# Recurrent mixer of a float32 transformer stack: products moved to GpSimd, decay scales folded into ScalarE's exponentials, one gate chunk moved behind the block products

## Chip, cores and metric

The kernel runs on one core of a Trainium2 chip. The metric is the device time of one launch in microseconds (us); three runs were timed, and lower is better.

## What is computed

A residual stream x of 256 positions by 1024 channels, float32, goes through a first block of two layers (an attention mixer with a convolutional feed-forward part, then a recurrent mixer with another such part) and through two layers of a second block. The change touches the recurrent mixer alone:

```
def odd_mixer(x, w_in, conv_w, conv_b, w_a, b_a, w_x, b_x, lam, w_out):
    gate_branch, xr = jnp.split(x @ w_in, 2, axis=-1)
    xr = causal_dwconv(xr, conv_w, conv_b)
    xb = xr.reshape(bsz, seq, RG_BLOCKS, RG_BLOCK_W)
    r = jax.nn.sigmoid(jnp.einsum('bsnc,ncd->bsnd', xb, w_a).reshape(bsz, seq, D_RNN) + b_a)
    i = jax.nn.sigmoid(jnp.einsum('bsnc,ncd->bsnd', xb, w_x).reshape(bsz, seq, D_RNN) + b_x)
    log_a = (-LRU_C * r.astype(jnp.float32)) * jax.nn.softplus(-lam.astype(jnp.float32))
    a = jnp.exp(log_a)
    u = jnp.sqrt(-jnp.expm1(2.0 * log_a)) * (i * xr).astype(jnp.float32)
    _, h = lax.associative_scan(lru_combine, (a, u), axis=1)
    y = h.astype(x.dtype) * jax.nn.gelu(gate_branch)
    return y @ w_out
```

## The kernel before

**Layout.** Channels lie on the 128 partitions, so an activation is 8 tiles of 128 by 256. Every operand of a matmul is split in two parts that TensorE takes in its fast float32 form: a rounded high part (written by ScalarE) and the low rest (written by VectorE). One product then takes three matmuls: high times high (line 247), high weights times low activation (line 248), low weights times high activation (line 249).

**The weight stream.** Weights come from HBM as a stream of 1 MB chunks (16 blocks of 128 by 128) in the order in which TensorE uses them. SyncE loads chunk n into one of three raw buffers as soon as the low part of chunk n-3 is written. ScalarE rounds it to `w_hi` (line 220, "high refill"), once the chunk four places ahead of it has been multiplied; VectorE writes `w_lo`, the difference (line 229, "low refill"). Both have a ring of four slots. Where these two refills stand in the order of ScalarE and VectorE is written out by hand; each engine runs its list in order and waits on semaphores.

**The stage around the change.** TensorE multiplies four chunks for the recurrent branch xr, one gate chunk (`od_gate0`), two chunks of block products (`od_ax`, eight steps j that give the arguments of r and i, each with two tiles), three more gate chunks and then the output projection `od_out`. Its first two chunks are taken together (`alternating`, lines 287 and 294): first all products with the high part of y, tile by tile as `yhi0` to `yhi3` come, then all with the low part (`ylo0` to `ylo3`). It waits at its start for the low refills of both chunks. VectorE scales the xr and gate products out of PSUM (line 314), adds three taps of the convolution (1431), writes the low part of the result (1437), multiplies r by the decay coefficient (1466, "la") and i by xr (1468, "ux"), finishes the argument of the root (1478, "v"), forms u (1486), scans (1491, two tiles for each pair h), multiplies by the gate (1497, "y") and takes the low part (1502, "ylo"). ScalarE has the last tap (1070), the high part of xr (1076), the sigmoids (1086), then for each pair of tiles Exp, Tanh and Square (1131, 1132, 1135), the roots (1138), the GELUs (1091) and the high part of y (1096, "yhi"). Each time another family of functions is needed, an ACT_TABLE_LOAD comes first. GpSimd does nothing in this stage; in the feed-forward parts of the first block it multiplies (760) and subtracts (766), in the second block it works at lines 1527 and 1530.

## Time and profile before

| quantity | value |
|---|---|
| median of 3 runs | 1929.05 us (1927.96 to 1929.65) |
| span of the profiled execution, first to last instruction | 1926.9 us |
| TensorE busy, matmuls | 1861.4 us (97%) |
| VectorE busy | 1394.7 us (72%) |
| ScalarE busy | 970.6 us (50%) |
| GpSimd busy | 141.2 us (7%) |
| mean granted TensorE clock | 0.984 of full speed |

The profile holds one execution. The page gives its span but no time of its own around that span; the median of the timed runs is 2.15 us longer than the span. Times in the rows are microseconds from the span's start. The recurrent mixer lies between about 386 and 478 us. PE is TensorE's matmuls, PEld its weight loads, DVE is VectorE, ACT is ScalarE, POOL is GpSimd. A row's idle time in brackets is what the engine spent waiting just before it, and on whom.

### The profile page before, as it was taken

What the parts mean: (1) busy time and instruction counts of PE and PEld (TensorE: products, weight loads), DVE (VectorE), ACT (ScalarE), POOL (GpSimd) and SP (SyncE); (2) the same over time, 40 slices, a digit from 0 to 9 for tenths busy, and PEclk for the clock granted to TensorE, in tenths of its full rate; (3) what the DMA queues carried; (4) which work ended last, traced back from release to release, by engine and by line L of the source; (5) the groups of instructions that cost most, each with busy time, mean ns of one, the idle gap of its engine ahead of it and who ended that gap; (6) DMA issues with size and microseconds to landing.
All of it is one profiled execution on the core that took longest, in us unless ns stands there. A gap on an engine that the chain in (4) does not pass through costs nothing.

```text
span 1926.9 us, 31805 instructions
## 1 busy us (share of the span) xinstructions
PE 1861.4 (97%) x13316; PEld 1749.7 (91%) x13316; DVE 1394.7 (72%) x1704; ACT 970.6 (50%) x1177; POOL 141.2 (7%) x128
## 2 busy tenths in 40 slices
PE   7978999998999999999999999999999999999997
PEld 7958999998999898889999988898889999998887
DVE  5796998578799557756775677757775686577774
ACT  5453755367665445544453455535554445355552
POOL 0020332000233000000300000000000020000000
PEclk9989999999999999999999999999999999999999
DMA  7413455534454445564455545553556345445551
GB/s 282 151 44 120 176 187 185 197 133 173 168 196 184 179 149 191 180 219 153 167 200 181 175 147 181 201 214 132 190 187 219 147 175 193 158 153 197 181 214 64
DMA packets 46788, 334.66 MB, mean 174 GB/s; under 512 B 5184, under 2 KB 5568, under 8 KB 6464
## 3 DMA queue, kind: packets, MB, share of 16 engines
q1 hardware_dynamic: 46512, 332.20, 47.9%
q8 instruction: 105, 1.72, 0.4%
q0 software_dynamic: 144, 0.52, 0.1%
q14 instruction: 27, 0.22, 0.0%
HBM read 331.65 MB, written 1.05 MB: 173 GB/s over the span
## 4 chain that ended last, share of the span: by engine, by line
PE 88%; DVE 7%; ACT 2%; DMA 1%; issue 1%; SPq 0%; DVEq 0%; ACTq 0%
PE psum L263 25%; PE psum L266 12%; PE psum L247 12%; PE psum L248 12%; PE psum L249 12%; PE psum L287 6%; PE psum L294 3%; DVE w_lo L229 2%; PE psum L334 1%; PE psum L506 1%; DMA w_raw<-stream_in 1%; PE psum L509 1%; PE psum L508 1%; PE psum L356 1%; DVE scratch L1318 0%
## 5 line engine op out<-in xcount | busy, mean ns | idle before, releaser
L220 ACT ACTIVATE w_hi<-w_raw 128x2048 fp32r<-128x2048 f32 x313 | 597.9, 1912 | 460.1 <-PE psum L249 223.7
L229 DVE TENSOR_TENSOR w_lo<-w_raw,w_hi 128x2048 fp32r<-128x2048 f32 x313 | 717.8, 2297 | 55.7 <-ACT w_hi L220 55.7
L247 PE MATMUL psum<-x_split,w_hi 128*128 128x256 f32 x1768 | 504.3, 285 | 10.7 <-DVE x_split L372 10.4
L248 PE MATMUL psum<-x_split,w_hi 128*128 128x256 f32 x1768 | 501.4, 284 | 0.0
L249 PE MATMUL psum<-x_split,w_lo 128*128 128x256 f32 x1768 | 501.4, 284 | 0.0
L263 PE MATMUL psum<-x_split,w_hi 128*128 128x512 f32 x1216 | 429.8, 399 | 0.0
L247 PEld LDWEIGHTS psum<-x_split,w_hi 128*128 128x128 f32 x1768 | 340.5, 193 | 12.0 <-issue 10.9
L266 PE MATMUL psum<-x_split,w_lo 128*128 128x256 f32 x1216 | 341.5, 281 | 0.0
L248 PEld LDWEIGHTS psum<-x_split,w_hi 128*128 128x128 f32 x1768 | 340.6, 193 | 0.1
L249 PEld LDWEIGHTS psum<-x_split,w_lo 128*128 128x128 f32 x1768 | 340.5, 193 | 0.0
L263 PE MATMUL psum<-h_split,w_hi 128*128 128x512 f32 x816 | 288.6, 399 | 0.0
L263 PEld LDWEIGHTS psum<-x_split,w_hi 128*128 128x128 f32 x1216 | 228.5, 188 | 57.0
L266 PEld LDWEIGHTS psum<-x_split,w_lo 128*128 128x128 f32 x1216 | 229.7, 189 | 0.0
L266 PE MATMUL psum<-h_split,w_lo 128*128 128x256 f32 x816 | 229.2, 281 | 0.0
L263 PEld LDWEIGHTS psum<-h_split,w_hi 128*128 128x128 f32 x816 | 153.3, 188 | 38.2
L266 PEld LDWEIGHTS psum<-h_split,w_lo 128*128 128x128 f32 x816 | 154.2, 189 | 0.0
L314 DVE TENSOR_TENSOR scratch<-psum,inv_rms 128x512 f32<-128x512 f32 (+1 forms) x129 | 87.0, 684 | 79.4 <-PE psum L249 79.2
L663 ACT ACTIVATE scratch<-psum 128x512 f32<-128x512 f32 x76 | 45.4, 598 | 195.0 <-PE psum L266 195.0
L247 PE MATMUL psum<-h_split,w_hi 128*128 128x256 f32 x480 | 138.9, 289 | 4.5 <-DVE h_split L1395 2.5
L249 PE MATMUL psum<-h_split,w_lo 128*128 128x256 f32 x480 | 137.3, 286 | 0.0
L248 PE MATMUL psum<-h_split,w_hi 128*128 128x256 f32 x480 | 137.3, 286 | 0.0
L308 DVE TENSOR_TENSOR scratch<-psum,scratch 128x512 f32<-128x512 f32 x76 | 52.6, 692 | 103.7 <-ACT scratch L663 103.7
(215 smaller groups left out, 2376.5 us busy)
## 6 DMA issues: line engine op xcount, KB each, us to landing
w_raw<-stream_in SPq DMA_DIRECT2D x313, 1024.0 KB, 4.8
x_resid<-x_in SPq DMA_DIRECT2D x1, 1024.0 KB, 6.9
y_out<-x_resid SPq DMA_DIRECT2D x4, 256.0 KB, 2.5
scratch<-mask_in SPq DMA_DIRECT2D x1, 768.0 KB, 11.0
scratch<-ev_in SPq DMA_DIRECT2D x1, 512.0 KB, 9.5
scratch<-inv_in POOLq DMA_DIRECT2D x1, 512.0 KB, 4.5
params<-par_in SPq DMA_DIRECT2D x1, 247.0 KB, 7.1
matrices<-mat_in SPq DMA_DIRECT2D x1, 192.0 KB, 8.9
```

Of the source, the lines that this page charges most:

```text
L220: act.activation(w_hi[:, n % RING, :], raw[:, n % RAWS, :], ACT.Copy).then_inc(hi_ready, 1)
L229: dve.tensor_tensor(w_lo[:, n % RING, :], raw[:, n % RAWS, :], w_hi[:, n % RING, :].bitcast(F32), ALU.subtract).then_inc(lo_ready, 1)
L247: pe.matmul(dst, w_hi[:, c.slot, b:b + P], src[:, k0 + k, 0, :], start=opens, stop=False)
L248: pe.matmul(dst, w_hi[:, c.slot, b:b + P], src[:, k0 + k, 1, :], start=False, stop=False)
L249: done = pe.matmul(dst, w_lo[:, c.slot, b:b + P], src[:, k0 + k, 0, :], start=False, stop=last and k == nk - 1 and m == len(tiles_) - 1)
L263: pe.matmul(ps[:, bank_, :], w_hi[:, c.slot, b:b + P], src[:, k0 + k, :, :].rearrange("p a t -> p (a t)"), start=first and k == 0, stop=False)
L266: done = pe.matmul(tile(bank_, 0), w_lo[:, c.slot, b:b + P], src[:, k0 + k, 0, :], start=False, stop=last and k == nk - 1)
L287: pe.matmul(tile(c.bank, m), w[:, c.slot, b:b + P], src[:, k0 + k, 0, :], start=k == 0 and m == 0 and w is w_hi, stop=False)
L294: done = pe.matmul(tile(c.bank, m), w_hi[:, c.slot, b:b + P], src[:, k0 + k, 1, :], start=False, stop=k == nk - 1 and m == 1)
L308: dve.tensor_tensor(dst, ps[:, c.bank:c.bank + 2, 0:T], S(ACC + 2 * c.slot, 2), ALU.add).then_inc(pair_taken, 2)
L314: dve.tensor_tensor(dst, bank(c.bank, tiles), rinv[:, :].unsqueeze(1).to_broadcast([P, tiles, T]), ALU.mult).then_inc(pair_taken, 1)
L663: act.activation(S(ACC + 2 * c.slot, 2), ps[:, c.bank:c.bank + 2, T:2 * T], ACT.Copy)\
```

## The change

Four things change, all in the recurrent mixer.

The gate chunk that stood ahead of the block products goes behind them, in the stream and in every engine's order, so there are now four `od_gate` chunks in a row. On VectorE the "la" multiplications go away: Exp and Tanh take the coefficient as a per-partition scale, one tile at a time, with two small extra operations that prepare the scales in the attention layer ahead. The "ux" products, three of the four "u" products and three of the four "ylo" subtractions go to GpSimd. And the refills are placed anew in the lists of ScalarE and VectorE.

```diff
-         ("od_xr", 4, 4), ("od_gate0", 1, 1), ("od_ax", 2, 0), ("od_gate", 3, 3), ("od_out", 4, 4),
+         ("od_xr", 4, 4), ("od_ax", 2, 0), ("od_gate", 4, 4), ("od_out", 4, 4),
...
@@ odd_act (ScalarE) @@
-            act.wait_ge(chunk_done, gate0.number + 1)
-            refill_hi(act, gate0)
             sigmoids(0)
...
-            refill_hi(act, Chunk("od_ax", 1))
             act.wait_ge(*A.after("i7"))
+            act.wait_ge(*ev_dve.after("l_pos"))
             for h in G4:
-                act.wait_ge(*od_dve.after(f"ux{2 * h + 1}"))
-                act.activation(S(TMP + 2 * h, 2), S(RR + 2 * h, 2), ACT.Exp).then_inc(*A.did(f"a{h}"))
-                act.activation(S(RR + 2 * h, 2), S(RR + 2 * h, 2), ACT.Tanh, scale=-1.0)\
-                   .then_inc(*A.did(f"tanh{h}"))
-                act.wait_ge(*A.after(f"a{h}"))
+                for j in (2 * h, 2 * h + 1):
+                    act.activation(S1(TMP + j), S1(RR + j), ACT.Exp, scale=small[:, 16 + j:17 + j])\
+                       .then_inc(*A.did(f"a{j}"))
+                    act.activation(S1(RR + j), S1(RR + j), ACT.Tanh, scale=small[:, 72 + j:73 + j])\
+                       .then_inc(*A.did(f"tanh{j}"))
+                act.wait_ge(*od_pool.after(f"ux{2 * h + 1}"))
+                act.wait_ge(*A.after(f"a{2 * h + 1}"))
                 act.activation(S(XC + 2 * h, 2), S(TMP + 2 * h, 2), ACT.Square).then_inc(*A.did(f"a2{h}"))
+                if h == 1:
+                    refill_hi(act, Chunk("od_ax", 1))
+                if h == 2:
+                    act.wait_ge(chunk_done, gate[0].number + 1)
+                    refill_hi(act, gate[0])
...
 VectorE, odd_dve
+            dve.wait_ge(*od_act.after("sqrt0"))
+            dve.wait_ge(*od_pool.after("ux1"))
+            dve.tensor_tensor(S(II, 2), S(II, 2), S(RR, 2), ALU.mult).then_inc(*V.did("u0"))
             scan(0)
-            take_scaled(dve, gate[1], S(GB + 4, 2))
+            take_scaled(dve, gate[2], S(GB + 4, 2))
             scan(1)
-            refill_lo(dve, gate[1])
             gated(0)
+            refill_lo(dve, gate[2])
+            scan(2)
             gated(1)
-            lo(0)
-            scan(2)
-            lo(1)
-            gated(2)
+            take_scaled(dve, gate[3], S(GB + 6, 2))
             scan(3)
-            take_scaled(dve, gate[2], S(GB + 6, 2))
-            lo(2)
+            gated(2)
             gated(3)
...
+        def odd_pool(pool):
+            for j in range(8):
+                pool.wait_ge(*od_act.after(f"i{j}"))
+                pool.tensor_tensor(S1(II + j), S1(II + j), S1(XC + j), ALU.mult).then_inc(*od_pool.did(f"ux{j}"))
+            for h in range(1, 4):
+                pool.wait_ge(*od_act.after(f"sqrt{h}"))
+                pool.wait_ge(*od_pool.after(f"ux{2 * h + 1}"))
+                pool.tensor_tensor(S(II + 2 * h, 2), S(II + 2 * h, 2), S(RR + 2 * h, 2), ALU.mult)\
+                    .then_inc(*od_pool.did(f"u{h}"))
+            for h in range(3):
+                pool.wait_ge(*od_act.after(f"yhi{h}"))
+                pool.tensor_tensor(hs[:, 2 * h:2 * h + 2, 1, :], S(GB + 2 * h, 2),
+                                   hs[:, 2 * h:2 * h + 2, 0, :].bitcast(F32), ALU.subtract)\
+                    .then_inc(*od_pool.did(f"ylo{h}"))
```

VectorE from the last root arguments (line 1478) to the first products of pair 0, in the program of before; 1486 is u, 1491 the scan, 314 a gate chunk taken out of PSUM, 229 a low refill, 1497 the product with the gate.

```order
L1478 SCALAR_TENSOR_TENSOR scratch<-scratch 128x512 x3
L1486 TENSOR_TENSOR scratch<-scratch 128x512
L1491 SCALAR_TENSOR_TENSOR scratch<-scratch 128x256 x2
L314 TENSOR_TENSOR scratch<-psum,inv_rms 128x512
L1486 TENSOR_TENSOR scratch<-scratch 128x512
L1491 SCALAR_TENSOR_TENSOR scratch<-scratch 128x256 x2
L229 TENSOR_TENSOR w_lo<-w_raw,w_hi 128x2048
L1497 TENSOR_TENSOR scratch<-scratch 128x512 x2
```

The same place in the changed program, where 1469 is the root argument, 1493 u of pair 0, 1482 the scan and 1488 the product with the gate.

```order
L1469 SCALAR_TENSOR_TENSOR scratch<-scratch 128x512 x2
L314 TENSOR_TENSOR scratch<-psum,inv_rms 128x512
L229 TENSOR_TENSOR w_lo<-w_raw,w_hi 128x2048
L1493 TENSOR_TENSOR scratch<-scratch 128x512
L1482 SCALAR_TENSOR_TENSOR scratch<-scratch 128x256 x2
L314 TENSOR_TENSOR scratch<-psum,inv_rms 128x512
L1482 SCALAR_TENSOR_TENSOR scratch<-scratch 128x256 x2
L1488 TENSOR_TENSOR scratch<-scratch 128x512
L229 TENSOR_TENSOR w_lo<-w_raw,w_hi 128x2048
```

A low refill now stands between the root arguments and u of pair 0, one u has left VectorE's list, and the other low refill (for the second chunk of the output projection) has moved from ahead of the first gate product to behind it.

ScalarE from the last sigmoids to the roots, in the changed program: 1085 is a sigmoid, 1128 Exp, 1130 Tanh, 1134 Square, 1142 the root, 220 a high refill.

```order
L1085 ACTIVATE scratch<-psum,params 128x256 x8
L1128 ACT_TABLE_LOAD
L1128 ACTIVATE scratch<-scratch,small 128x256
L1130 ACTIVATE scratch<-scratch,small 128x256
...
L1134 ACTIVATE scratch<-scratch 128x512
L220 ACTIVATE w_hi<-w_raw 128x2048
...
L1142 ACT_TABLE_LOAD
L1142 ACTIVATE scratch<-scratch 128x512 x4
```

Before, one high refill stood ahead of the table load and none between Exp and the roots; now none is ahead and two lie inside (behind pair 1 and behind pair 2), and sixteen operations on 128 by 256 take the place of eight on 128 by 512.

GpSimd between its last subtraction of one feed-forward part and its first product of the next, in the changed program.

```order
L766 TENSOR_TENSOR h_split<-scratch,h_split 128x256
L1514 TENSOR_TENSOR scratch<-scratch 128x256 x8
L1518 TENSOR_TENSOR scratch<-scratch 128x512 x3
L1522 TENSOR_TENSOR h_split<-scratch,h_split 128x2x256 x3
L760 TENSOR_TENSOR scratch<-scratch 128x256 x2
```

The fourteen rows of lines 1514 (ux), 1518 (u1 to u3) and 1522 (ylo0 to ylo2) are new there; before, line 760 followed upon line 766.

## Rows read from the trace of the kernel before

**Rows 1.** The page, busy time of each engine: us, share, instructions.

```profile
PE 1861.4 (97%) x13316; PEld 1749.7 (91%) x13316; DVE 1394.7 (72%) x1704; ACT 970.6 (50%) x1177; POOL 141.2 (7%) x128
```

**Rows 2.** Waits, 396 to 475 us: us in total, times, longest.

```profile
PE psum L287 <- ACT h_split L1096: 5.8, 2, 5.4
PE psum L247 <- issue: 2.0, 1, 2.0
```

**Rows 3.** Windows: stretch, length, busy of each engine, granted PE clock, DMA share, GB/s.

```profile
163.10:166.40 3.30, 3.30 (x18) 3.30 (x17) 2.75 (x17) 0.00 (x0) 0.00 (x0) 0.50 0.51 164
...
423.60:427.00 3.40, 3.40 (x28) 3.40 (x29) 2.71 (x3) 3.40 (x8) 0.00 (x0) 1.00 0.38 154
...
452.20:456.60 4.40, 4.36 (x20) 4.39 (x21) 4.33 (x8) 3.37 (x4) 0.00 (x0) 0.50 0.58 223
```

**Rows 4.** Timeline of PE: start, length, instruction, [idle before <-releaser].

```profile
161.82 0.39 PE L247 MATMUL psum<-h_split,w_hi 128*128 128x256 f32 x1 [2.50 <-DVE h_split L1395]
...
409.89 0.28 PE L247 MATMUL psum<-x_split,w_hi 128*128 128x256 f32 x1
...
423.59 0.35 PE L247 MATMUL psum<-h_split,w_hi 128*128 128x256 f32 x1 [2.02 <-issue]
...
429.42 0.28 PE L247 MATMUL psum<-x_split,w_hi 128*128 128x256 f32 x1
...
452.24 0.55 PE L287 MATMUL psum<-h_split,w_hi 128*128 128x256 f32 x1 [5.38 <-ACT h_split L1096]
...
460.52 0.39 PE L287 MATMUL psum<-h_split,w_hi 128*128 128x256 f32 x1 [0.38 <-ACT h_split L1096]
```

**Rows 5.** Timeline of ACT.

```profile
420.88 1.90 ACT L220 ACTIVATE w_hi<-w_raw 128x2048 fp32r<-128x2048 f32 x1
...
427.85 3.07 ACT L1086 ACTIVATE scratch<-psum,params 128x256 f32<-128x256 f32 x8
432.59 1.92 ACT L220 ACTIVATE w_hi<-w_raw 128x2048 fp32r<-128x2048 f32 x1 [1.67 <-DMA w_raw<-stream_in]
...
441.57 0.62 ACT L1135 ACTIVATE scratch<-scratch 128x512 f32<-128x512 f32 x1
442.20 1.28 ACT L1138 ACT_TABLE_LOAD   x1
...
459.83 0.63 ACT L1096 ACTIVATE h_split<-scratch 128x512 fp32r<-128x512 f32 x1 [0.76 <-DVE scratch L1497]
...
468.15 0.89 ACT L367 ACTIVATE x_split<-x_resid,params 128x256 fp32r<-128x256 f32 x2
```

**Rows 6.** Timeline of DVE.

```profile
414.66 0.69 DVE L1437 TENSOR_TENSOR h_split<-scratch,h_split 128x512 fp32r<-128x512 f32 x1
...
421.03 2.45 DVE L1431 SCALAR_TENSOR_TENSOR scratch<-scratch,params 128x255 f32<-128x255 f32 x6
...
444.16 0.69 DVE L1486 TENSOR_TENSOR scratch<-scratch 128x512 f32<-128x512 f32 x1 [1.25 <-ACT scratch L1138]
...
448.56 2.27 DVE L229 TENSOR_TENSOR w_lo<-w_raw,w_hi 128x2048 fp32r<-128x2048 f32 x1
...
466.33 0.69 DVE L565 TENSOR_TENSOR x_resid<-psum,x_resid 128x512 f32<-128x512 f32 x1 [2.94 <-PE psum L294]
```

**Rows 7.** Timeline of POOL and DVE in other stages, where both work.

```profile
930.73 2.28 DVE L229 TENSOR_TENSOR w_lo<-w_raw,w_hi 128x2048 fp32r<-128x2048 f32 x1
...
930.76 3.40 POOL L1530 TENSOR_TENSOR scratch<-scratch 128x512 f32<-128x512 f32 x1
937.89 1.29 POOL L1527 TENSOR_TENSOR scratch<-scratch 128x512 f32<-128x512 f32 x1 [3.73 <-DVE scratch L1564]
...
938.32 3.00 DVE L229 TENSOR_TENSOR w_lo<-w_raw,w_hi 128x2048 fp32r<-128x2048 f32 x1
...
502.99 3.24 DVE L712 SCALAR_TENSOR_TENSOR scratch<-scratch,params 128x255 f32<-128x255 f32 x8
...
504.22 2.61 POOL L760 TENSOR_TENSOR scratch<-scratch 128x256 f32<-128x256 f32 x1 [176.46 <-ACT scratch L641]
```

More of the change, by code:

```diff
@@ L1062, in odd_act @@
             xr = [Chunk("od_xr", g) for g in G4]
-            gate0 = Chunk("od_gate0", 0)
-            gate = [Chunk("od_gate", g) for g in range(3)]
+            gate = [Chunk("od_gate", g) for g in G4]
             def last_tap(g):
@@ L1416, in odd_dve @@
             xr = [Chunk("od_xr", g) for g in G4]
-            gate0 = Chunk("od_gate0", 0)
-            gate = [Chunk("od_gate", g) for g in range(3)]
+            gate = [Chunk("od_gate", g) for g in G4]
             def branch(g):
@@ L1480, in odd_dve @@
                 if h == 0:
-                    take_scaled(dve, gate[0], S(GB + 2, 2))
+                    take_scaled(dve, gate[0], S(GB, 2))
+                if h == 1:
                     refill_lo(dve, gate[0])
+            take_scaled(dve, gate[1], S(GB + 2, 2))
+            refill_lo(dve, gate[1])
             def scan(h):
-                dve.wait_ge(*od_act.after(f"sqrt{h}"))
-                dve.tensor_tensor(S(II + 2 * h, 2), S(II + 2 * h, 2), S(RR + 2 * h, 2), ALU.mult)\
-                   .then_inc(*V.did(f"u{h}"))
-                dve.wait_ge(*V.after(f"u{h}"))
+                dve.wait_ge(*(od_pool.after(f"u{h}") if h else V.after("u0")))
                 for k in range(2):
@@ L1696, in _ @@
             up_pool(pool, "up0", FF1, U["up0"], 0)
+            odd_pool(pool)
             up_pool(pool, "up1", FF1, U["up1"], 0)
@@ L1931, in pack_stream @@
     pairs(w, [(8 + 2 * g, 9 + 2 * g) for g in range(4)])
-    pairs(w, two[:1])
     wa, wx = i["od_w_a"][0], i["od_w_x"][0]
@@ L1940, in pack_stream @@
         put(np.concatenate(part, axis=1))
-    pairs(w, two[1:])
+    pairs(w, two)
     pairs(i["od_w_out"][0], two)
```

68 lines of the change are left out of this document (28 added, 40 removed).

## The prediction, written before the changed kernel ran

> **What bounds the kernel now.** The page comes first: TensorE is busy 97% of the span, GpSimd 7% [rows 1]. So a change gains only where TensorE stands still, and the waits of the stretch say where that is: 5.4 us in one piece for the high part of y, another 0.4 us for the same, and 2.0 us among the block products [rows 2]. The timeline places them: 2.02 us before 423.59, 5.38 before 452.24, 0.38 before 460.52 [rows 4]. The windows add a cost that no wait shows: from 452.20 to 456.60 the granted clock is 0.50 (1.2 GHz), after the 5.38 us in which TensorE did nothing, and 20 matmuls fill 4.36 us; at 1.00 (2.4 GHz) 28 fill 3.40 [rows 3]. That is 0.22 against 0.12 us each, so 1.9 us lost. All in all 9.7 us of 1929: the most that any change to this stage could give.
>
> What the large gap waits for: TensorE is done with the gate chunks at 446.86 (452.24 less 5.38) and needs both `yhi0` and the low refill of the second chunk. The refill ends at 450.83 (448.56 + 2.27 [rows 6]), `yhi0` at about 452.1. Both hang on ScalarE's chain of Exp to roots, then on VectorE's chain from u of pair 0 (444.16 [rows 6]) on. The end of the stage is VectorE's first eviction at 466.33, which waited for TensorE [rows 6]. I follow the change to this point; behind it the waits of these rows move as one piece, and TensorE has no gap of its own that could take a delay back soon.
>
> **Part 1, block products and sigmoids.** The xr chunks end at 409.9 [rows 4]; a chunk is 48 matmuls, 5.76 us. The block products start early now, but steps 2 and 3 need the low part that VectorE writes at 414.66 + 0.69 = 415.35 [rows 6], so step 3 ends near 418.3. Step 4 needs its bank emptied by the sigmoids of step 0. ScalarE's refill at 420.88 (1.90 us [rows 5]) no longer stands in front of them, so these end near 421.7 and step 4 starts at 421.8. The convolution of pair 3, six taps of 2.45 us [rows 6], loses the refill ahead of it and ends by 422, so its low part is there at about 423.8, before step 6. Steps 4 to 7 end at 421.8 + 5.8 = 427.6, against 429.42 [rows 4]. The gate chunks, now four, end at 427.6 + 23.0 = 450.6. The last sigmoids end at 429.3: ScalarE is free for them at 426.3 (its refill of 1.9 stays ahead), and eight take 3.07 [rows 5]. Before, they ended at 427.85 + 3.07 = 430.9.
>
> **Part 2, Exp to roots.** Before: 1.67 us of waiting for the weights' DMA, refill 1.92, a table load and twelve operations on 128 by 512, to 442.2; table load 1.28; first root done at about 444.1 [rows 5]. After: table load 1.28; sixteen operations on 128 by 256 with a pointer as scale, two of which take 0.89 (0.40 each, overlap taken off) [rows 5], 6.4; four squares of 0.52 (0.62 less overlap), 2.1; two refills of 1.8 inside, 3.6. From 429.3 that gives 442.7, so the first root is 0.5 us later. Exp itself is not shown in that form. Its bounds: half of the 512-column operation, 0.26 (2.2 us less in all), and the undisturbed length of the pointer form, 0.49 (1.4 us more). I take 0.40, since that row has both the columns and the pointer.
>
> **Part 3, VectorE behind the roots.** Before, it waited 1.25 us for the root and began u at 444.16 [rows 6]. After, v3 (443.4), a gate chunk out of PSUM (444.0) and a low refill of 2.28 come first, so it is free at 446.2: 2.1 us later. From u to the second scan pair it took 448.56 - 444.16 = 4.4 us [rows 6]; one u (0.6) leaves that stretch and the gate product (0.7) joins it. So y0 would be done at 446.2 + 4.5 = 450.7 with nothing else. The "la" products (8) and the five that GpSimd takes gave VectorE's time back in a stretch where it waited anyway, or pay here only as that one u.
>
> **Part 4, the collisions.** Where VectorE and GpSimd work at the same time, each waits for the other. GpSimd's 128 by 512 subtraction takes 1.29 us alone (as line 1527) and 3.40 when it is issued 0.03 us after a low refill of 2.28: it ends 1.15 behind it. The reverse: a refill issued 0.43 us into a GpSimd operation of 1.29 takes 3.00, not 2.28, and so ends 2.15 behind that operation's end [rows 7]. GpSimd's u1, u2 and u3 become ready together at 445 to 446, beside the refill; if the two take turns, all three get in before y0, at 1.1 us each: 3.3. So y0 is done at 454.0, the low refill that follows at 456.2, and the output projection starts at 456.3, 4.1 later than 452.24. Then VectorE has two scans, y1, a gate chunk, two scans and y2, 4.3 us, and ylo0 and ylo1 get in between, 2.2: y2 at 462.7. The high part is 0.63 [rows 5], TensorE takes pair 2 at 463.4 and needs 3.84 for the rest of the high pass and 3.84 for the low one (32 matmuls each): 471.1. Before, that point was 466.3 to 466.4. Sum: +4.7. The ux products collide as well (eight, among three refills in a row), but the chunks that these refills serve are needed 1 to 7 us later, so they are free here.
>
> The Trainium skill ("SBUF — State Buffer", SBUF: two separate sides) says that the two engines share one pair of ports as an exclusive lock, held for a whole instruction, whichever comes first. By that rule each operation of GpSimd is a full turn and the sum is the same +4.7. One row speaks against it, and it makes rival 1.
>
> **Part 5, the clock.** TensorE now stands still for about 3.5 us before step 4 (418.3 to 421.8). After 2.50 us the clock was 0.50 for a while [rows 3, 4], after 2.02 us it stayed at 1.00 [rows 3, 4]. So I expect a half-speed stretch of 3.3 us: up to 1.5 us more for the block products, of which the end of the sigmoids, and with it all that follows, sees about half: +0.6 (bounds 0 and 1.5). The half-speed stretch at the start of the output projection comes again, but its 16 matmuls then wait for y1 anyway; that is in the sum. The two extra scale operations cost VectorE 0.4 us in the attention stage, while TensorE has work queued: 0, at most 0.4. The change keeps the number of matmuls and bytes.
>
> **Sum.** +4.7 + 0.6 = +5.3 on the trace's own time (1926.9 span, 2.15 below the median). Two overlaps of 0.1 that I rounded against VectorE leave +5.1, on the median 1934.2.
>
> **Rivals.**
>
> 1. *VectorE keeps the ports.* The eight taps from 502.99 ran without a break (3.24 us) while a GpSimd product issued at 504.22 waited 2.0 us, to their end [rows 7]. If so, u1 gets in only at the PSUM read (0.5 us lost), y0 is done at 451.3, u2 after the refill (1.1), u3 at the next PSUM read (0.6): y2 at 459.3, the end at about 468.5. +2.2: 1931.3. For it: this row. Against: row 930.76 and its like, where GpSimd got its turn at the first end.
> 2. *The ports cost nothing* (not slower). Then y0 at 450.7, refill at 452.9, y2's high part at 458.3 behind ScalarE's refill and GELU, end 458.4 + 7.7 = 466.1: -0.2, with the clock term up to +0.4: 1928.9. It decides against "slower" when the five collisions cost under about 0.85 us each in place of 1.1. Against it: both engines' rows in [rows 7].
> 3. *The clock falls again* in the gaps of about 1.5 us that the output projection now has before y1 and y2, so its last 64 matmuls run at half speed for 3.4 us more: +1.5 to +2: 1936.0. For it: the stretch is idle for half its time. Against: at 423.60 a gap of 2.02 did nothing [rows 3].
> 4. *Faster.* The chains are ready when TensorE ends its gate chunks at 450.6: end 450.6 + 7.7 + 3.84 = 462.2, 1924.9. It needs y0 and the low refill 2.3 us earlier than in rival 2, so Exp at its lower bound (2.2 us) and free ports together.
>
> **How the numbers follow.** Turns with the ports, my forecast, 0.53; rival 1 0.14; rival 2 0.14; rival 3 0.13; rival 4 0.06. The forecast is 1934.2. Range: from rival 2 less its rounding (1928.5) to the forecast with the clock's upper bound and part of rival 3 (1936.8). A change of 0.2% (3.9 us) is about what a measurement of this kernel can tell. The forecast lies 1.2 us above that bound, with Exp's price and the clock able to take it below: 0.42 of its 0.53 count as slower, with rival 3 0.13 and 0.03 from rival 1, so slower 0.58; faster 0.06; same 0.36.
>
> **What would show it.** In the changed profile: step 4 of the block products near 421.8 and a clock of 0.50 behind it; Exp and Tanh at about 0.49 us each; the first root near 444.6 to 445.3; a GpSimd product at line 1518 of 1.3 to 2 us with single scans of over 1 us beside it; the output projection starting at 456 to 457 on the low refill, not on yhi0; first eviction near 471. Short scans throughout would be rival 2; GpSimd rows of over 2 us with short scans, rival 1. Wrong in another way would be a wait that I put at nothing: the refills behind ux, or the attention stage.

## The result and the profile after

The changed kernel takes 1937.36 us (median of 5 runs, 1933.44 to 1939.48), the kernel before in the same comparison 1929.45 (1927.96 to 1931.04): ratio 1.0039, interval 1.0028 to 1.0050. It is slower, as forecast, and by more than the forecast of 1934.2 and its upper end of 1936.8. With seven more runs in later comparisons the median of twelve is 1936.1 (1931.79 to 1939.48). The kernel before had its median between 1928.68 and 1929.33 there (two of its runs, at 3018 and 3642 us, were slow ones and are left out). So the loss is about 6.9 us in twelve runs, 7.9 in the first five, and the median of twelve lies inside the forecast's range, which that of the first five left by 0.6 us.

The page, busy time of each engine: GpSimd has 14 instructions more than in [rows 1], VectorE is hardly relieved.

```profile
PE 1865.9 (96%) x13316; PEld 1752.9 (91%) x13316; DVE 1393.5 (72%) x1684; ACT 973.7 (50%) x1185; POOL 164.1 (8%) x142
```

Waits of TensorE, 409 to 473 us (in total, times, longest), beside [rows 2]: 4.8 us ahead of the output projection in place of 5.4, but now for VectorE's low refill; 3.3 us for a sigmoid ahead of step 4 of the block products; 1.0 us for the high part of pair 2.

```profile
PE psum L287 <- DVE w_lo L229: 4.8, 1, 4.8
PE psum L247 <- ACT scratch L1085: 3.3, 1, 3.3
PE psum L247 <- DVE h_split L1442: 2.3, 2, 2.0
PE psum L287 <- ACT h_split L1095: 1.0, 1, 1.0
```

Windows (stretch, length, busy of each engine, granted clock of TensorE, DMA share, GB/s), beside [rows 3]: steps 4 to 7 of the block products run wholly at 0.50, which is 1.2 GHz of 2.4.

```profile
421.50:427.60 6.10, 6.07 (x28) 6.10 (x29) 5.06 (x4) 5.74 (x12) 5.58 (x4) 0.50 0.13 34
427.60:453.00 25.40, 25.40 (x214) 25.40 (x212) 16.91 (x13) 23.15 (x37) 11.81 (x8) 1.00 0.53 200
...
458.00:461.80 3.80, 3.78 (x18) 3.66 (x19) 3.80 (x6) 1.19 (x2) 1.35 (x2) 0.55 0.70 246
```

Timeline of TensorE, beside [rows 4]: step 0 of the blocks, which waits 2.04 us here; step 4, which waits for a sigmoid; the output projection; its third pair.

```profile
411.84 0.36 PE L247 MATMUL psum<-h_split,w_hi 128*128 128x256 f32 x1 [2.04 <-DVE h_split L1442]
...
421.53 0.55 PE L247 MATMUL psum<-h_split,w_hi 128*128 128x256 f32 x1 [3.25 <-ACT scratch L1085]
...
458.02 0.36 PE L287 MATMUL psum<-h_split,w_hi 128*128 128x256 f32 x1 [4.76 <-DVE w_lo L229]
...
464.71 0.39 PE L287 MATMUL psum<-h_split,w_hi 128*128 128x256 f32 x1 [1.02 <-ACT h_split L1095]
```

Timeline of ScalarE, beside [rows 5]: the last two sigmoids, the table load, the first Exp and Tanh with a pointer as scale (0.42 us from one start to the next here, 0.40 behind), the four roots.

```profile
430.26 0.84 ACT L1085 ACTIVATE scratch<-psum,params 128x256 f32<-128x256 f32 x2 [0.60 <-PE psum L249]
431.12 1.28 ACT L1128 ACT_TABLE_LOAD   x1
432.41 0.51 ACT L1128 ACTIVATE scratch<-scratch,small 128x256 f32<-128x256 f32 x1
432.83 0.49 ACT L1130 ACTIVATE scratch<-scratch,small 128x256 f32<-128x256 f32 x1
...
445.92 2.19 ACT L1142 ACTIVATE scratch<-scratch 128x512 f32<-128x512 f32 x4
```

Timeline of VectorE, beside [rows 6]: v of pair 3, gate chunk and low refill; u0; scans (L1482); y0 (L1488); the low refill that releases the output projection; the first eviction (L565).

```profile
444.64 0.69 DVE L1469 SCALAR_TENSOR_TENSOR scratch<-scratch 128x512 f32<-128x512 f32 x1 [3.15 <-ACT scratch L1134]
445.25 0.68 DVE L314 TENSOR_TENSOR scratch<-psum,inv_rms 128x512 f32<-128x512 f32 x1
445.85 2.28 DVE L229 TENSOR_TENSOR w_lo<-w_raw,w_hi 128x2048 fp32r<-128x2048 f32 x1
448.05 1.79 DVE L1493 TENSOR_TENSOR scratch<-scratch 128x512 f32<-128x512 f32 x1
449.88 3.30 DVE L1482 TENSOR_TENSOR_SCAN scratch<-scratch 128x256 f32<-128x256 f32 x2
453.11 0.66 DVE L314 TENSOR_TENSOR scratch<-psum,inv_rms 128x512 f32<-128x512 f32 x1
453.69 1.26 DVE L1482 TENSOR_TENSOR_SCAN scratch<-scratch 128x256 f32<-128x256 f32 x2
454.87 0.66 DVE L1488 TENSOR_TENSOR scratch<-scratch 128x512 f32<-128x512 f32 x1
455.45 2.28 DVE L229 TENSOR_TENSOR w_lo<-w_raw,w_hi 128x2048 fp32r<-128x2048 f32 x1
457.65 2.34 DVE L1482 TENSOR_TENSOR_SCAN scratch<-scratch 128x256 f32<-128x256 f32 x2
...
472.45 0.69 DVE L565 TENSOR_TENSOR x_resid<-psum,x_resid 128x512 f32<-128x512 f32 x1 [3.67 <-PE psum L294]
```

Timeline of GpSimd over the same stretch, beside [rows 7]: u1 to u3, then the low part of pair 0.

```profile
447.15 5.49 POOL L1518 TENSOR_TENSOR scratch<-scratch 128x512 f32<-128x512 f32 x3 [13.23 <-ACT scratch L1142]
456.27 2.60 POOL L1522 TENSOR_TENSOR h_split<-scratch,h_split 128x512 fp32r<-128x512 f32 x1 [3.63 <-ACT h_split L1095]
```

Read the last two lists side by side. While GpSimd has u1 to u3, VectorE's u0 takes 1.79 us (0.69 alone, [rows 6]) and two scans 3.30; as soon as GpSimd is done (452.64), two scans take 1.26. GpSimd's low part was ready at 456.27, waited for the refill to end at 457.73 and took its turn of 1.14 us; a scan that was issued at 457.65 waited for that. The first eviction is 6.1 us later than before (472.45 against 466.33). From the start of the roots to the output projection it is 12.10 us here (445.92 to 458.02); the second and third profiles have 12.07 and 12.06. This stretch is used below, since it varies less than the whole stage.

### The profile page after: what moved, and what is told of

It is laid out like the page before. It is cut to its first block, busy times and chain, and to the rows that moved or that the text cites. A ratio compares the mean times of both kernels' runs of the same rounds, so it can differ in the third digit from the quotient of the medians.

```text
span 1935.4 us, 31815 instructions
## 1 busy us (share of the span) xinstructions
PE 1865.9 (96%) x13316; PEld 1752.9 (91%) x13316; DVE 1393.5 (72%) x1684; ACT 973.7 (50%) x1185; POOL 164.1 (8%) x142
## 4 chain that ended last, share of the span: by engine, by line
PE 87%; DVE 8%; ACT 2%; DMA 1%; issue 1%; SPq 0%; DVEq 0%; ACTq 0%
PE psum L263 25%; PE psum L266 12%; PE psum L247 12%; PE psum L248 12%; PE psum L249 12%; PE psum L287 6%; PE psum L294 3%; DVE w_lo L229 2%; PE psum L334 1%; DMA w_raw<-stream_in 1%; PE psum L506 1%; ACT w_hi L220 1%; PE psum L509 1%; PE psum L508 1%; PE psum L356 1%
```

## The experiments

The time from the end of the xr chunks (where the 2.04 us wait begins) to the first eviction is called the stage; for kernels that keep a gate chunk in between it is counted from step 2 of the block products (423.59 in [rows 4]). Every median is of 8 to 11 runs (6 for the changed kernel and fill_step4; the third profile of the changed kernel and the second of before come with one run each), against the kernel before on the same chip: 1929.2 to 1929.3, and 1928.7 for fill_both and the first run of the reordered kernel. The intervals of the ratios are 0.09% (1.7 us) to each side or a little more.

| kernel | median us | against before | stage against before |
|---|---|---|---|
| changed, second and third profile | 1936.10; 1931.87 (one run) | +6.9; +3.2 | +4.0; +5.0 (first profile +6.2) |
| products_back | 1933.15 | +3.9 | +4.6 |
| ux_only | 1933.22 | +4.0 | +2.2 |
| fill_step4 | 1935.58 | +6.4 | +4.2 |
| fill_both | 1934.85 | +6.2 | +4.2 |
| low_refill_early | 1932.72 | +3.4 | +3.5 |
| products_only | 1930.87 | +1.5 | +1.8 |
| scales_only | 1931.09 | +1.8 | +2.3 |
| gate_move_only | 1930.42 | +1.1 | -0.1 |
| delay20; delay41 | 1932.17; 1934.33 | +2.9; +5.0 | +0.1; 0.0 |
| refill_moved; refill_fill | 1927.85; 1927.38 | -1.4; -1.9 | -0.8; -0.8 |
| reordered, twice | 1927.30; 1927.30 | -1.4; -2.0 | -1.6; -0.5 |
| reordered_fill | 1926.26 | -3.1 | -3.0 |

**The changed kernel again.** No edit.

> The changed kernel once more, for a second profile. The first profile of it shows 6.1 us more at the first eviction of the output projection (472.45 against 466.33) and 8.3 us more from 1118 us on; the 2.2 us between come from stretches at half the granted clock, 6.8 and 10.2 us long where the profile of before has 3.4 and 6.8. Theory: those 2.2 us are how the stretches happened to fall in one execution; the stage's 6.1 us recur within 0.5 us, the 2.2 us do not (between -3.5 and +3.5 here). Rival: they follow from the change of this stage and recur within 0.5 us. The median should lie within 3 us of 1937.4.

1936.10 us, ratio 1.0032 (1.0020 to 1.0044). Its profile has the same span as the first, 1935.4, but it lost the time in other places: step 4 follows a wait of 2.21 us, the first eviction is at 469.98, and at the end of a later layer TensorE runs 10.2 us at half speed:

```profile
421.32 0.36 PE L247 MATMUL psum<-h_split,w_hi 128*128 128x256 f32 x1 [2.21 <-issue]
...
469.98 0.69 DVE L565 TENSOR_TENSOR x_resid<-psum,x_resid 128x512 f32<-128x512 f32 x1 [3.66 <-PE psum L294]
```

The last line below is that stretch; the two ahead of it are the half-speed stretches among the block products and around the start of the output projection:

```profile
412.70:416.10 3.40, 3.40 (x18) 3.40 (x18) 3.40 (x6) 2.31 (x3) 0.00 (x0) 0.50 0.12 48
453.60:460.40 6.80, 4.86 (x23) 4.89 (x24) 6.80 (x7) 2.91 (x4) 4.12 (x2) 0.50 0.47 154
...
1726.80:1737.00 10.20, 7.98 (x36) 7.63 (x37) 7.94 (x19) 4.35 (x10) 0.00 (x0) 0.50 0.00 0
```

Both theories had it wrong: neither the 6.1 us in the stage nor the 2.2 us behind it recurred as such. The stage lost 4.0 (counted from its own start) and the part behind it 4.8.

**The products back on VectorE.**

```diff
-        od_pool = Steps(sem("od_pool"), [f"ux{j}" for j in range(8)] + ["u1", "u2", "u3", "ylo0", "ylo1", "ylo2"])
...
-                dve.wait_ge(*(od_pool.after(f"u{h}") if h else V.after("u0")))
+                dve.wait_ge(*od_act.after(f"sqrt{h}"))
+                dve.tensor_tensor(S(II + 2 * h, 2), S(II + 2 * h, 2), S(RR + 2 * h, 2), ALU.mult)\
+                   .then_inc(*V.did(f"u{h}"))
```

> The changed kernel with all 14 products of GpSimd back on VectorE (ux between the low refills, u1 to u3 ahead of their scans, the low parts of y in the order of before). Theory, the two engines take turns and each of the five or six products costs VectorE 1.1 us or more: VectorE now does six more products at 0.65 to 0.69 us and loses the turns; y0 at about 451.4 in place of 455.5, y2 at about 461.1 in place of 464.0, first eviction near 469.4 in place of 472.45, so about 3 us less than the changed kernel (1934.3), still 3 us over before. Rival, the collisions cost little and the rest of the change (the low refill ahead of u0, ScalarE's 16 short exponentials) makes the loss: no gain, or 1 to 2 us more than the changed kernel.

1933.15 us: 3 us less than the changed kernel, as the theory of turns had it, though VectorE now does 14 products more. The two intervals overlap a little; the next kernel, with 11 runs of its own, repeats the median, and the rows show the gain directly. Its u0 takes 0.68 us and the first two scans 1.27, in place of 1.79 and 3.30, and from the roots to the output projection it is 9.65 us in place of 12.1. Its waits are 2.3 us for the low refill, then 0.8 and 2.1 for high parts of y. In this one profile the stage is as long as in the changed kernel (61.0 against 60.4 to 62.7 us), since it has a half-speed stretch of 3.4 us in its last, TensorE-bound part; the gain shows in the rows above and in the median, not in the stage of that profile.

**Only the ux products on GpSimd.** The edit is the same for u1 to u3 and the low parts; ux stays.

> The changed kernel with u1 to u3 and the low parts of y back on VectorE; only the eight ux products stay on GpSimd, where they fall among three low refills. Theory, their collisions are free, since nothing waits soon for what these refills serve: the same time as with all products back, within 1 us. Rival, they are not free: 1 to 2 us slower than with all products back, seen as the last sigmoids, the first root or the start of the gate chunks coming later.

1933.22 us, 0.1 us from all products back: their collisions are free, as expected. So the price is that of u1 to u3 and of the low parts.

**TensorE kept busy ahead of step 4.**

```diff
+                    if j == 4:
+                        pe.wait_ge(pair_taken, Chunk("od_gate", 0).event + 1)
+                        for _ in range(26):
+                            pe.matmul(tile(Chunk("od_gate", 0).bank, 0), w_hi[:, c.slot, 0:P], xs[:, 0, 0, :],
+                                      start=True, stop=True)
```

> The changed kernel with 26 matmuls of 128 by 256 that nothing uses, put ahead of step 4 of the block products, into a free bank, where TensorE stood still for 3.25 us and the granted clock then was 0.50 for 6.8 us. The results are those of the reference. Theory, the clock term of the forecast (0.6 us) was the step that was too small: TensorE now works through the wait, the clock stays at 1.00 through steps 4 to 7, they end at about 427.6, the sigmoids at 429.3 to 429.6 in place of 431.1, and all behind it comes 1.5 us sooner: 1935.9. Rival, the half speed costs nothing here because ScalarE's sigmoids set the end: sigmoids at 430.5 or later and less than 0.5 us gained.

Its window over steps 4 to 7 has 54 matmuls at 1.00 where the changed kernel had 28 at 0.50:

```profile
421.40:427.60 6.20, 6.20 (x54) 6.20 (x54) 5.17 (x5) 6.20 (x14) 5.44 (x4) 1.00 0.10 16
```

The table load for Exp follows step 0 by 17.3 us (429.23 less 411.98); in the first profile of the changed kernel by 19.3 (431.12 less 411.84). By that pair half speed cost 2.0 us there, where I had counted 0.6 and 1.5 at most. But in the second profile of the changed kernel, without a filler, it is 17.0 (428.67 less 411.63): the clock fell for 3.4 us earlier, at 412.7, behind the 2.04 us wait ahead of step 0. It did so in this kernel's profile too (3.4 us from 412.4), so the filler ahead of step 4 did not keep the whole stretch at 1.00. The stage is 2.0 us shorter than in the first profile, and no shorter than in the second. The median, 1935.58, is 0.5 us below that of the changed kernel: less than the 1.5 expected, and not told apart from nothing.

**One part alone.** Three kernels on the one before: the products on GpSimd; the scales in ScalarE's exponentials; the gate chunk behind the blocks.

```diff
+            for h in range(1, 4):
+                pool.wait_ge(*od_act.after(f"sqrt{h}"))
+                pool.tensor_tensor(S(II + 2 * h, 2), S(II + 2 * h, 2), S(RR + 2 * h, 2), ALU.mult)\
```

> The kernel before with one part of the change alone: GpSimd takes the eight ux, u1 to u3 and the low parts of y 0 to 2; decay scales stay on VectorE, the gate chunks and refills where they were. Theory: u1 to u3 fall on VectorE's scans and on its refill ahead of y0 and cost 1.1 us each, the two low parts another 2.2 ahead of y2; taken off are the u's and low parts that VectorE no longer does (0.6 each, five of them ahead of y2). About +2.7 at y0 and +2.5 to +3.1 at y2: 1932.2, near the 3.5 us by which the changed kernel gained when its products went back. Rival: before a root is there VectorE is not late in this kernel, so the products cost under 1 us here, and the changed kernel's loss needs the parts together.

1930.87 us, +1.5 (ratio 1.0007, 0.9998 to 1.0016), half of what was expected. TensorE waits 7.2 us for the high part of y in place of 5.4, so the first three collisions are there (the first two scans take 3.30 us); TensorE then waits for nothing more, so the low parts cost nothing visible in this order. By the medians the same products cost twice as much in the changed kernel (3.0 us) as in the one before, as the rival would have it; with intervals of about 2 us to each side the runs do not show it.

```diff
-                act.activation(S(TMP + 2 * h, 2), S(RR + 2 * h, 2), ACT.Exp).then_inc(*A.did(f"a{h}"))
+                for j in (2 * h, 2 * h + 1):
+                    act.activation(S1(TMP + j), S1(RR + j), ACT.Exp, scale=small[:, 16 + j:17 + j])\
+                       .then_inc(*A.did(f"a{j}"))
```

> The kernel before with the decay scales in ScalarE's exponentials alone (sixteen operations on 128 by 256 with a pointer as scale at 0.40 us in place of eight on 128 by 512 at 0.52; VectorE's eight scale products left out). Theory: 16 x 0.40 - 8 x 0.52 = 2.2 us more on the chain from Exp to the roots, on which the stage waits here, so +2.2 at the first root, the output projection and the end: 1931.5. Rival: VectorE's lighter list gives part of it back: under +1.

1931.09 us, +1.8 (1.0011, 1.0002 to 1.0020). TensorE's wait grows from 5.4 to 7.6 us, by the 2.2 that was worked out, and the stage by 2.3:

```profile
PE psum L287 <- ACT h_split L1096: 7.6, 1, 7.6
PE psum L247 <- issue: 2.0, 1, 2.0
```

```diff
-         ("od_xr", 4, 4), ("od_gate0", 1, 1), ("od_ax", 2, 0), ("od_gate", 3, 3), ("od_out", 4, 4),
+         ("od_xr", 4, 4), ("od_ax", 2, 0), ("od_gate", 4, 4), ("od_out", 4, 4),
```

> The kernel before with the gate chunk behind the block products and the refills' new places alone; products and decay scales as before. It is the kernel with all products back, with the eight long exponentials again. Theory: the first root 2.2 us earlier (near 442.8), but VectorE is then held by the low refill of the second gate chunk until about 444.4, against 446.5 with all products back, so y0, the output projection and the end come 2.1 us earlier than there: 1931.0. Rival: the roots do not matter behind that refill and the time is that of all products back, 1933.2.

1930.42 us, +1.1 (1.0006, 0.9997 to 1.0015), 0.6 us under what was expected. The stage is as long as before: TensorE's wait ahead of the output projection is down to 0.6 us, and it waits 2.9 for high parts of y instead.

```profile
PE psum L287 <- ACT h_split L1095: 2.9, 2, 2.1
PE psum L247 <- issue: 2.2, 1, 2.2
PE psum L247 <- DVE h_split L1437: 2.0, 1, 2.0
PE psum L287 <- DVE w_lo L229: 0.6, 1, 0.6
```

The three parts add to 4.4 us; together they cost 6.9 by the medians, 4.0 to 6.2 by the stages. With three such intervals in the sum it stays open whether the parts cost more together than alone.

**The low refill ahead of v3.**

```diff
             for h in G4:
 
+                if h == 3:
+                    take_scaled(dve, gate[1], S(GB + 2, 2))
+                    refill_lo(dve, gate[1])
                 dve.wait_ge(*od_act.after(f"a2{h}"))
...
-            take_scaled(dve, gate[1], S(GB + 2, 2))
-            refill_lo(dve, gate[1])
```

> The changed kernel with one step of VectorE moved: the second gate chunk's take and the low refill behind it (2.28 us) stand ahead of v of pair 3, in the time in which VectorE waits 3 us for ScalarE's Square, and no longer between v3 and u0. It tests the 2.1 us by which the prediction had VectorE late behind the roots. Theory: u0 starts with the first root, about 1.5 us earlier, and y0, the output projection and the end with it: 1935.2. Rival: the GpSimd products then fall on the scans and fill the time won, under 0.5 us.

The stage is 60.0 us, 1.5 less than the mean of the three of the changed kernel (61.5), as expected, and 0.4 less than the shortest of them. From the roots to the output projection it is 9.97 us (444.22 to 454.19) in place of 12.1: the 2.1 us of Part 3. VectorE's timeline shows why: the refill fills an idle time, and u0 starts on the root, with 0.69 us alone.

```profile
440.82 2.29 DVE L229 TENSOR_TENSOR w_lo<-w_raw,w_hi 128x2048 fp32r<-128x2048 f32 x1
443.03 0.68 DVE L1472 SCALAR_TENSOR_TENSOR scratch<-scratch 128x512 f32<-128x512 f32 x1
444.89 0.69 DVE L1494 TENSOR_TENSOR scratch<-scratch 128x512 f32<-128x512 f32 x1 [1.17 <-ACT scratch L1142]
```

The median fell by more, to 1932.72. Its runs lie in two groups: five from 1930.88 to 1931.34, four from 1937.80 to 1938.58, with mean granted clocks of 0.984 to 0.985 and of 0.980; one lies between, at 1934.10. A median that falls between two groups says little about 2 us.

**A pure delay.** Is the time behind the stage the same whatever the stage takes? Matmuls that nothing uses, in a place where TensorE never waits:

```diff
+                if ph == "up1" and c.n == 8:
+                    for _ in range(41):
+                        pe.matmul(tile(c.bank, 0), w_hi[:, c.slot, 0:P], xs[:, 0, 0, :], start=True, stop=True)
```

> The kernel before with 20 matmuls of 128 by 256 that nothing uses, ahead of chunk 8 of the second convolved FFN (near 560 us), where TensorE never waits: a pure delay of 20 x 0.12 = 2.4 us behind the stage in question. Theory A, as the prediction had it, all that follows moves as one piece: the median rises by 2.4 us (1931.6) and the mean granted clock stays at the 0.984 of before. Theory B, a shift changes how long the half-speed stretches at the later stage boundaries are: the median differs from +2.4 by over 1 us, to either side, the clock leaves 0.984 and the runs spread over more than the 4 us of before.

> The same with 41 such matmuls: 4.9 us of pure delay, near to what the changed kernel loses in its stage. Theory A: 1934.1 with a mean clock of 0.984 and a spread as before. Theory B: the median differs from that by over 1 us and the clock from 0.984; if it is like the changed kernel (1936.7 over eleven runs, mean clock 0.982), about 1936 to 1937.

+2.9 for 2.4 us and +5.0 for 4.9 (ratios 1.0019 and 1.0031): a shift alone costs itself. The median clock was 0.983, and two runs of each fell to 0.980 or 0.981 and took 2.5 to 5 us more than the median, so theory B holds in part; but it does not explain a median 2 us too high.

**Second profile of before, third of after.**

> The kernel before once more, for a second profile. In the first, the time from the first eviction of the output projection (466.33) to the end is 1460.6 us and holds 38.7 us of half-speed stretches. Theory, the length of these stretches goes with the kernel: the sum recurs within 4 us and the rest within 1 us. Rival, chance: they differ by 7 us or more of half speed, and the rest by 2 us or more.

> The changed kernel a third time. So far the stage ended 6.1 and 3.7 us later than before and the rest took 2.4 and 4.8 us longer, with 45.5 and 53.6 us at half speed. Theory, by kernel: 45 us or more at half speed behind the stage and a rest of 1462.5 or more. Rival, chance: anything from 35 us on.

The two profiles of before agree: from the first eviction to the end it is 1460.6 and 1460.7 us, with 38.8 us at half speed in both. The three of the changed kernel have 1463.0, 1465.4 and 1459.2 us, with 45.6, 53.8 and 31.9 (where the expectations have the same sums, they are 0.1 to 0.2 lower by rounding). In each, 11.4 to 12.8 us of that are a last stretch that starts as the last matmuls run and delays next to nothing. Without it, before has 27.3 us twice, and the changed kernel 34.1, 41.0 and 20.5.

The time behind the stage follows these numbers. Over all twenty profiles of this document (the two delay kernels less their added 2.4 and 4.9 us) it grows by 0.31 us for each us at half speed, from 1459.2 at 20.5 to 1465.4 at 41.0, and no profile lies more than 0.6 us off that line. So what the changed kernel lost or won behind the stage is half-speed time.

Windows over the same code in a later layer, first of the second profile of before, then of the third of the changed kernel:

```profile
1722.50:1732.70 10.20, 8.41 (x68) 8.14 (x68) 9.89 (x22) 6.54 (x13) 0.00 (x0) 1.00 0.00 0
```

```profile
1726.00:1736.20 10.20, 8.41 (x69) 8.12 (x68) 9.87 (x22) 6.52 (x13) 0.00 (x0) 1.00 0.00 0
```

Both do 68 or 69 matmuls in 10.2 us; the second profile of the changed kernel did 36 (above). So the half-speed stretches differ from run to run in the changed kernel, and hardly in the one before: of 126 timed runs of before 109 had a mean clock of 0.983 to 0.985, of twelve of the changed kernel four had.

**TensorE busy in both waits.** The filler of fill_step4, and 38 such matmuls ahead of the output projection.

> The changed kernel with matmuls that nothing uses in both long waits of the stage: 26 ahead of step 4 of the block products and 38 (4.6 us) ahead of the output projection. The results are those of the reference. Theory: the granted clock stays at 1.00 from the block products to the end of the stage but for what the 2 us ahead of them do; the stage ends 1.5 to 2 us sooner than in the changed kernel, mostly at the block products, since the output projection waits for the high parts of y anyway: 1935. If standing still in the stage is also what makes the later half-speed stretches longer, the mean clock is 0.984 or more and the time 1933; if not, it is 0.982 to 0.983.

The stage is 60.6 us, the same as with the first filler alone: what the second one saved in clock, the high parts of y took back, as expected. That is 2.0 us less than in the changed kernel's first profile and 0.9 less than the mean of three. The time is 1934.85 us. The nine runs spread from 1931.02 to 1938.64, with mean clocks from 0.981 to 0.989. So standing still ahead of step 4 and of the output projection is not what makes the later half-speed stretches vary. The 2.04 us ahead of step 0 are left in this kernel, with 3.4 us at half speed at their end in this profile (from 413.2, step 0 at 413.31).

**What the explanation asks for.** First ScalarE's refill alone, moved in the kernel before as the change moves it; then the same with 26 matmuls ahead of the output projection.

```diff
-            refill_hi(act, Chunk("od_ax", 1))
             act.wait_ge(*A.after("i7"))
...
                 act.activation(S(XC + 2 * h, 2), S(TMP + 2 * h, 2), ACT.Square).then_inc(*A.did(f"a2{h}"))
+                if h == 1:
+                    refill_hi(act, Chunk("od_ax", 1))
```

> The kernel before with one part of the change alone: ScalarE's refill of the high part for the second block chunk stands behind the Square of pair 1, not ahead of the table load of Exp, where it waited 1.67 us for its weights. Products, decay scales and gate chunks stay as they were. Theory: the chain from Exp to the roots starts 3.5 us earlier, pays the refill's 1.9 inside, so the first root and all behind it come 1.6 to 1.9 us sooner: output projection at about 450.5, first eviction near 464.5, 1927.2 to 1927.6. Rival: the low refill that waits for this high one, or the clock, takes it back: within 0.5 us of before.

> The kernel before with that refill moved, and 26 matmuls of 128 by 256 that nothing uses (3.1 us) between the last gate chunk and the output projection, so that TensorE does not stand still there for more than about 0.5 us. The results are those of the reference. Theory: the clock stays at 1.00 at the start of the output projection, but its matmuls then wait for the high parts of y, so the stage ends within 0.3 us of the kernel with the refill moved alone; what can be gained is only a shorter sum of half-speed stretches, up to 1 us. Rival: the high parts of y are there in time and the full 1.9 us that half speed costs in these rows come back.

1927.85 (0.9994, 0.9985 to 1.0003) and 1927.38 (0.9995, 0.9986 to 1.0004): 1.4 and 1.9 us less than before, within what a comparison can tell from nothing. The table load for the roots came 17.8 us after step 2 of the blocks, 18.6 before (440.69 less 422.85, 442.20 less 423.59): 0.8 us gained in place of 1.6 to 1.9, since a half-speed stretch at 424.4 held up the last sigmoids by 1.0 us. With the filler the stage is as long as without (-0.8), as expected. Its edit:

```diff
+            pe.wait_ge(*od_act.after("i7"))
+            for _ in range(26):
+                pe.matmul(tile(4, 0), xs[:, 0, 0, 0:P], xs[:, 0, 0, :], start=True, stop=True)
```

Then the gate move with the low refill ahead of v3, as above, GELU of pair 3 ahead of ScalarE's refill, and VectorE's list reordered. The cut shows the list against the kernel with the gate move alone:

```diff
             gated(1)
-            lo(0)
+            gated(2)
             take_scaled(dve, gate[3], S(GB + 6, 2))
             scan(3)
-            lo(1)
-            gated(2)
-            lo(2)
             gated(3)
-            lo(3)
+            for h in G4:
+                lo(h)
```

> The gate move alone (products on VectorE, decay scales as before), with three moves that the explanation asks for: the take of the second gate chunk and its low refill ahead of v of pair 3, y of pair 2 right behind y of pair 1, and all low parts of y behind y of pair 3, with ScalarE's GELU of pair 3 and its refill placed to match. Theory: VectorE is no longer held by the low refill behind the roots (1.3 to 1.5 us), and high parts 2 and 3 of y, for which TensorE waited 2.13 us, come 3 us sooner, so the output projection follows the gate chunks with under 1 us of waiting and the first eviction is near 463.0 to 463.5, against 466.24 with the gate move alone and 466.33 before; the clock stays at 1.00 there. 1926.0, or up to 1 us less by the clock. Rival: the low refills or the low parts of y are late in their turn and the time stays at 1929 to 1930.

> The reordered kernel once more, timed anew. Theory: the stage is 1.6 us shorter than before from the end of the xr chunks to the first eviction (54.9 against 56.4 us), and the median lies 1 to 2 us below before, too little for the interval to leave 1 in one comparison. Rival: the 1.4 us of the first comparison were chance, and the median is within 0.5 us of before.

> The reordered kernel with 17 matmuls that nothing uses (2.0 us) ahead of step 4 of the block products. The results are those of the reference. Theory: no half-speed stretch near 422, steps 4 to 7 and the gate chunks end about 1 us sooner, but the output projection then waits for VectorE's low refill, which does not move: first eviction 0 to 0.5 us sooner, median within 0.7 us of the reordered kernel. Rival: a full 1 us or more of gain, or a loss, through the later half-speed stretches.

The reordered kernel took 1927.30 twice, against 1928.68 and 1929.33 (ratios 0.9996, 0.9987 to 1.0005, and 0.9989, 0.9980 to 0.9998). Its waits show the explanation at work: the 5.4 us ahead of the output projection of [rows 2] are gone, and of those for high parts 0.8 is left (first profile; the second has the same 0.8, but 6.8 us at half speed from 420.3 and a stage of 55.9 us in place of 54.9).

```profile
PE psum L247 <- issue: 2.2, 1, 2.2
PE psum L247 <- DVE h_split L1437: 2.0, 1, 2.0
PE psum L287 <- ACT h_split L1095: 0.8, 1, 0.8
```

With 17 matmuls in the 2.2 us wait it took 1926.26 (0.9983, 0.9974 to 0.9992), the only one whose whole interval lies well below 1: 3 us under the kernel before and 10 under the changed one. Its expectation was beaten: the stage got 1.4 us shorter than in the first profile of the reordered kernel, not 0 to 0.5, and the median 1.0 us shorter, not within 0.7. The intervals of the two kernels overlap, so that the filler itself gains is likely and not shown.

## Why the prediction was right and where it failed

**Right: the turns at the ports (Part 4).** The rows show one turn for each operation, in the order of issue, as [rows 7] had them. Rival 1 (VectorE keeps the ports) is out: u1 to u3 took 5.49 us together and each VectorE instruction beside them 1.65 to 1.79. Rival 2 (free ports) is out by the same rows: beside GpSimd u0 took 1.79 us and without it 0.68; and the products' return gave 3 us back. A gate chunk's take, which has one input in PSUM, is not held up: in the kernel with the low refill ahead of v3 it kept its 0.66 us while GpSimd had u3 (up to 450.02).

```profile
448.86 0.66 DVE L314 TENSOR_TENSOR scratch<-psum,inv_rms 128x512 f32<-128x512 f32 x1
```

```profile
445.45 4.57 POOL L1519 TENSOR_TENSOR scratch<-scratch 128x512 f32<-128x512 f32 x3 [12.06 <-ACT scratch L1142]
```

The rule of the Trainium skill ("SBUF — State Buffer", SBUF: two separate sides), by which the pair of ports is held for a whole instruction and VectorE needs it when both of its inputs lie in SBUF, agrees with both. The row from 502.99, on which rival 1 rested, stays unexplained.

What I counted as five turns at 1.1 us ahead of y2 gave a stage of +4.7; three profiles measured +6.2, +4.0 and +5.0, mean 5.1, against 5.3 with the clock term. That this is so close is in part luck, since the three spread over 2.2 us.

**Right: step by step, up to the gate chunks.** Step 4 at 421.8, measured 421.53, 421.32 and 420.96. Exp and Tanh 0.49 us long and 0.40 apart, as taken. VectorE free at 446.2; measured 448.1 (445.85 + 2.28) and, in the second and third profiles, 445.7 and 446.3: the low refill stands ahead of u0 as Part 3 said, and moved away it gave 2.1 us back up to the output projection and 1.5 in the stage. The output projection at 456.3; measured 458.02, 455.54 and 456.19.

**Wrong: Part 5, the size of the clock term, in the stage.** "+0.6 (bounds 0 and 1.5)" was 2.2 in the first profile, 1.1 in the third and 0 in the second, by the time from step 0 to the end of the sigmoids (19.3, 18.1 and 17.0 us). I had taken one length of the half-speed stretch, 3.3 us, from one row; steps 4 to 7 were at 0.50 throughout in the first profile. It also priced only one of the two waits among the block products. TensorE stands still for 2.04 us ahead of step 0 as well, and in the second and third profiles a half-speed stretch began behind that (412.7 and 412.0). Of the twelve profiles of kernels with the gate move, nine have one that begins at 411.3 to 413.4, at the end of that wait or shortly behind it. In the other three TensorE waited 3.25 us ahead of step 4 in place of 2.2, and was at half speed there.

**Wrong: "behind it the waits of these rows move as one piece".** This is the step that put the time of the first five runs outside the range, together with the clock term above: the profiled one of them, at that median, had +6.2 in the stage and +2.4 behind it. The stage's sum was within 0.3 us of the mean of three profiles; the rest of the kernel, which I had not touched and took as fixed, was 2.4 and 4.8 us longer in two profiles and 1.4 shorter in the third. The timed runs say the same without a profile: at a mean clock of 0.985 the changed kernel took 1933.4 (two runs) against 1928.2 (25 runs of before), +5.2; at 0.983 it took 1935.0 and 1935.5 against 1929.7 (39 runs), +5.6; and half of its runs had 0.982 or less. The remaining 1.8 us of the 6.9 fit the 1.9 us by which the three profiles were longer behind the stage on average, all of it half-speed time (0.31 us for each us of it). Rival 3 put half speed in the second half of the output projection; in the first profile it came at its start (458.0 to 461.8), so it did not go that way either.

**Right in sign: the chances.** Slower by over 0.2% had 0.58. The upper end of the range, 1936.8, was made of the stage's terms alone and had no room for the clock elsewhere.

**Open.** Why the changed kernel's half-speed stretches vary from run to run and those of before hardly do. Not the shift alone (delay41), nor TensorE standing still ahead of step 4 or of the output projection (fill_both). Of the kernels with the gate move, the reordered one had 0.984 or more in 20 of 22 runs, so it is not the gate move alone, nor that wait alone, which the reordered kernel has too.

## What to carry to other kernels

Take work off an engine only where that engine is late: VectorE's eight scale products and eight ux products stood where it waited anyway, and the products that were handed over at the tight place cost it 1.1 us each where they had cost 0.6. Before work leaves a list, look for an idle stretch in the list itself: one refill moved up by 5 us made the stage 1.5 us shorter, fourteen products moved away lost 3 by the medians. And where a sum rests on one profile, price the clock with a second one: two profiles of one kernel with equal spans lost the time in different places here.

## What the runs showed of the hardware

A wait of about 2.0 us left the granted clock at 1.00 in the first profile of the changed kernel (411.84, clock 1.00 to 417) and was followed by 3.4 us at 0.50 in the second (412.70); nine of the twelve profiles that have this wait have such a stretch at its end or within 1.3 us behind it. Behind the 2.02 us wait of the kernels that keep the gate chunk in between (423.59 in [rows 4]) two of eight profiles have such a stretch (refill_moved and refill_fill, from 424.4 and 424.0). At one place of a later layer, the changed kernel had 10.2 us at 0.50 in the second profile and none in the third. In the changed kernel 0.001 of mean clock goes with about 1.0 us of time (1939.4 at 0.980, 1931.8 at 0.987 and 0.988). Matmuls that nothing uses, in a wait that the program cannot avoid, kept the clock at 1.00 (54 matmuls in 6.20 us); in the reordered kernel they went with a median 1.0 us lower, within what its intervals leave open.
